# A two-block transformer step: the gated branch's score products in four parts, three of them inside the dense round that follows

## The chip, the cores and the metric

The kernel runs on one core of a Trainium2 chip. The metric is the device time of one execution, in microseconds. Full clock of TensorE is 2.4 GHz, and the profile gives the granted share of it.

## The reference

A first block (modulated norm, one input projection, a gated linear recurrence and a windowed attention side by side, output projection, 32-expert feed-forward with four experts a token) is followed by a second block of another kind. All in float32, 256 tokens, width 1024. The change touches only the gated recurrence of the first block, which works on chunks of 64 tokens and 4 heads of 128 keys:

```python
def step(state, inp):
    qc, kc, vc, lfc = inp
    b = jnp.cumsum(lfc, axis=-2)
    o_inter = jnp.einsum('bhck,bhkv->bhcv', qc * jnp.exp(b), state)
    rel = b[:, :, :, None, :] - b[:, :, None, :, :]
    decay = jnp.exp(jnp.where(causal, rel, -jnp.inf))
    scores = jnp.einsum('bhik,bhjk,bhijk->bhij', qc, kc, decay)
    o = o_inter + jnp.einsum('bhij,bhjv->bhiv', scores, vc)
    b_last = b[:, :, -1:, :]
    new_state = jnp.exp(b_last[:, :, 0, :])[..., None] * state + jnp.einsum(
        'bhjk,bhjv->bhkv', kc * jnp.exp(b_last - b), vc)
    return new_state, o
```

## The kernel before

Every engine has its own hand-written instruction stream, and semaphores join them. The dense projections of block 1 are *rounds* 0 to 15. A float32 weight is split into an upper part, made by ScalarE (`split_upper`, L356), and a lower part, made by VectorE (`split_lower`, L361); a matmul of the projection is then three products of rounded operands. Weights come in *pieces*. A round that is cut by columns has two pieces, j = 0 and j = 1, of 256 columns each; round 7 has pieces 13 and 14, round 8 has 15 and 16. Within a piece `split_cols` goes over two column groups c of 128, and for each over 8 contraction tiles and 3 products, so a round is 2 x 2 x 24 = 96 matmuls of 128x256. There are three places for upper parts, so ScalarE can make piece 16 only when TensorE has used piece 13.

Between rounds TensorE does the small work of the two branches, in the banks 4 to 6 of PSUM, taken in turn by `aux_bank()`. The consumer of each such bank waits on the count `aux_done`, and gives the bank back with `aux_free_V` or `aux_free_A`. Consumers take the banks in the order in which TensorE fills them.

The stretch of the change, on TensorE: the attention's value products; the gated branch's *score products* (64 products, for g in 8, i in 4, par in 2, each with 16 moving columns and 16 to 64 stationary columns, all into one bank, with one increment of `aux_done` behind the last); round 7; the transposes of the decayed keys (L1643, two banks); the products that make the chunk states (three banks, each waiting for `hg_kdT`); round 8; the products of scores and values.

The same stretch on VectorE, in order: the attention output (L2141, L2142), the gate (L2148, L2149), `split_lower(14)`, a memset of `st` (L2155), the masking of the scores from PSUM into `st` (L2161, 8 instructions, which waits for the scores' `aux_done`) with a memset that frees the bank (L2164), `split_lower(15)`, `split_lower(16)`, two copies of the transposed keys (L2170, `hg_kdT`) each with a memset (L2172), the states (L2178, L2181). `st` is first read by TensorE after round 8.

ScalarE makes the upper parts 15 and 16 in this stretch, then applies the sigmoid to the result of round 7 (L498) and makes the upper part 17. SyncE loads the weights; many of its loads wait for TensorE to be done with the slot (`big_done`, and in the expert stage `m1_up_done`, L989). Matmuls of float32 are recorded twice each in the profile; nearly all are recorded at the helper's line L563.

Of the kernel before, what the change touches and what calls it, by code (L numbers as in the profile page):

```python
# [31 lines left out]
CH, SUB = 64, 16  # L32
# [79 lines left out]
def program(nc, t, out):  # L112
    ctx = ExitStack()
    with ctx:
# [5 lines left out]
        def S(name):  # L120
            if name not in sems:
                sems[name] = ctx.enter_context(nc.semaphore(name))
            return sems[name]
# [31 lines left out]
        def at(m, name, lo=0, n=None, mem=arena):  # L155
            a, w = m[name]
            a = int(a * KB) + lo
            return mem[:, a:a + (n if n else int(w * KB) - lo)]
# [185 lines left out]
        hT_up = hT_r[:, :, :]  # L344
        hT_low = ring2_r[:, 1, 2048:4096].rearrange("p (k t) -> p k t", k=KD)
# [12 lines left out]
        def split_lower(v, n):  # L358
            v.wait_ge(S("w_upper"), n + 1)
            _, _, w, w_r = PIECES[n]  # L360
            nc.vector.tensor_tensor(w_r, w, upper(n), ALU.subtract).then_inc(S("w_lower"), 1)  # L361
# [75 lines left out]
        def banks(r):  # L437

            return slice(5, 7) if r == 0 else slice(2 * (r % 2), 2 * (r % 2) + 2)

        def kt_view(i):

            lo = 8 * SUB * i * (i + 1)
            return at(A1MAP, "kt", lo, 256 * (i + 1)).rearrange("p (g j) -> p g j", g=16)
# [117 lines left out]
        def mm(o, w, m, first, last):  # L562
            return nc.tensor.matmul(o, w, m, start=first, stop=last)  # L563
# [38 lines left out]
        def router_mm(w, ne, i, ks):  # L602
            for k in ks:
                last = mm(PS[:, 4 + i, 0:ne], hT[:, k, i * P:(i + 1) * P], w[:, k, :], k == 0, k == KD - 1)
            return last
# [836 lines left out]
        def _(pe):  # L1442
            aux = [0]

            def aux_bank():

                r = aux[0]
                aux[0] += 1
                if r >= 3:
                    wait(pe, aux_free(r - 3))  # L1450
                return PS[:, 4 + r % 3, :]

            def split_products(r, product, up, lo, ready, between=None):

                if r >= 2:
                    wait(pe, round_free(r - 2))
                ns = pieces_of(r)
                for j, n in enumerate(ns):
                    pe.wait_ge(S("w_lower"), n)
                    if ready:  # L1460
                        pe.wait_ge(S(ready), j + (1 if r < R2 else 3))
                    wu, wl = upper(n), PIECES[n][3]
                    last = product(j, ((up[j], wl), (lo[j], wu), (up[j], wu)), j == 0, j == len(ns) - 1)
                    last.then_inc(S("big_done") if j == len(ns) - 1 else S("half_done"), 1)
                    if between and j == 0:
                        between()
# [35 lines left out]
                                          n == 0 and m == 0 and k == 0, n == 1 and m == 2 and k == 3)  # L1502
                    last.then_inc(S("big_done") if n else S("half_done"), 1)

            def split_cols(r, up=hT_up, lo=hT_low, between=None):

                o = PS[:, banks(r), :].rearrange("p b (c t) -> p (b c) t", c=2)

                def product(j, parts, first, last):
                    nk, nc_ = parts[0][1].shape[1], parts[0][1].shape[2] // P  # L1510
                    for c in range(nc_):
                        for k in range(nk):
                            for m, (a, w) in enumerate(parts):
                                ins = mm(o[:, nc_ * j + c, :], w[:, k, c * P:(c + 1) * P], a[:, k, :],
                                         k == 0 and m == 0, k == nk - 1 and m == 2)
                    return ins
                split_products(r, product, (up, up), (lo, lo), None, between)

# [27 lines left out]
            for c in range(4):  # L1546
                last = nc.tensor.transpose(PS[:, 4, c * P:(c + 1) * P], modrow[:, 0, c * P:(c + 1) * P], ident)
# [5 lines left out]
            split_tokens(1)  # L1553
            keep_warm_short(6, 4)
            split_cols(2)
            ada(5)
            ada(6)
            split_cols(3)

            pe.wait_ge(S("consts"), 16)  # L1560
# [3 lines left out]
            for r in range(3):  # L1564
                o = aux_bank()
                for j in range(2):
                    for i in range(TT):
                        last = nc.tensor.transpose(o[:, (2 * j + i) * P:(2 * j + i + 1) * P], qk[:, i, 2 * r + j, :], ident)
# [5 lines left out]
            def att_score(o, hh, qtile, keys):  # L1574
                q = slice(64 * (hh % 2), 64 * (hh % 2) + 64)
                return mm(o, qkT[q, hh // 2, qtile * P:(qtile + 1) * P], qkT[q, 4 + hh // 4, 0:keys], True, True)


            o = [aux_bank() for _ in range(2)]
            for j in range(4):  # L1580
                for r in range(2):
                    last = att_score(o[r][:, j * P:(j + 1) * P], 2 * j + r, 0, P)
# [4 lines left out]
            for g in range(2):  # L1587
                o = [aux_bank() for _ in range(2)]
                for j in range(2):
                    for r in range(2):  # L1590
                        last = att_score(o[r][:, j * 256:(j + 1) * 256], 4 * g + r + 2 * j, 1, 256)
                        if j == 1:
                            last.then_inc(S("aux_done"), 1)
            split_tokens(5)
            ada(9)
            split_cols(6)
            ada(10)

            s = at(A1MAP, "s").rearrange("p (h n) -> p h n", h=AH)
            pe.wait_ge(S("att_p"), 1)  # L1600
            for b in range(3):
                for r in range(2):
                    o = aux_bank()
                    for j in range(4):
                        last = nc.tensor.transpose(o[:, j * P:(j + 1) * P], s[:, 4 * r + j, b * P:(b + 1) * P], ident)  # L1605
# [8 lines left out]
            for r in range(2):  # L1614
                o = aux_bank().rearrange("p (m t) -> p m t", m=2)
                for j in range(4):
# [3 lines left out]
                    last = mm(o[q, j // 2, P:256], vv[:, 1, kv], pT1[:, hh, :], False, True)  # L1620
# [2 lines left out]
            pe.wait_ge(S("hg_scores_in"), 1)  # L1623
            o = aux_bank().rearrange("p (g i) -> p g i", g=8)
            qt = at(A1MAP, "qt").rearrange("p (g i) -> p g i", g=16)
            for g in range(8):
                for i in range(4):
                    n = SUB * (i + 1)
                    for par in range(2):
                        hc, q0 = 2 * g + par, 64 * par  # L1630
                        last = mm(o[q0:q0 + n, g, SUB * i:SUB * i + SUB], kt_view(i)[:, hc, :],
                                  qt[:, hc, SUB * i:SUB * i + SUB], True, True)
            last.then_inc(S("aux_done"), 1)
            split_cols(7)

            pe.wait_ge(S("hg_kd"), 1)
            kd = at(A1MAP, "b").rearrange("p (h t) -> p h t", h=HH)
# [2 lines left out]
            for i in range(TT):  # L1640
                o = aux_bank()
                for hh in range(HH):
                    last = nc.tensor.transpose(o[:, hh * P:(hh + 1) * P], kd[:, hh, i * P:(i + 1) * P], ident)  # L1643
                last.then_inc(S("aux_done"), 1)

            for c in range(3):
                i, q = c // 2, slice(64 * (c % 2), 64 * (c % 2) + 64)
                o = aux_bank()
                pe.wait_ge(S("hg_kdT"), i + 1)
                for hh in range(HH):  # L1650
                    last = mm(o[:, hh * P:(hh + 1) * P], kdT[q, i, hh, :], vals[q, i, hh, :], True, True)
# [7 lines left out]
            for i in range(TT):  # L1659
                o = aux_bank()  # L1660
                pe.wait_ge(S("hg_state"), 2 * i + 1)
                halves = [(2 * i + par, slice(64 * par, 64 * par + 64)) for par in range(2)]
                for hh in range(HH):
                    for c, q in halves:
                        last = mm(o[q, hh * P:(hh + 1) * P], st[q, hh, i, :], vals[q, i, hh, :], True, c == 0)
                    for c, q in halves:
                        if c:
                            last = mm(o[q, hh * P:(hh + 1) * P], qb[:, hh, c * CH:(c + 1) * CH], states[:, c - 1, hh, :],
                                      False, True)
# [3 lines left out]
            o = aux_bank()  # L1673
            for c in range(4):
                last = nc.tensor.transpose(o[:, c * P:(c + 1) * P], modrow[:, 1, c * P:(c + 1) * P], ident)
# [4 lines left out]
            for r in range(2):  # L1680
                o = aux_bank()
                for j in range(2):
                    for i in range(TT):
                        last = nc.tensor.transpose(o[:, (2 * j + i) * P:(2 * j + i + 1) * P], ho[:, i, 2 * r + j, :], ident)
# [19 lines left out]
            for i in range(TT):  # L1704
                pe.wait_ge(S("hT_A"), 3 + i)
                last = router_mm(w_r1, NE, i, range(4, KD))
# [6 lines left out]
            for part in range(2):  # L1713
                for i in (part, part + 2):
                    for k in range(2):
                        c = P * k + CAP * (i // 2)
                        for tile in range(TT):
                            last = mm(PS[:, part, c:c + CAP], h[:, tile, 256 * i + k:256 * i + 256:2],
                                      selS[:, tile * CAP:(tile + 1) * CAP], tile == 0, tile == TT - 1)
# [66 lines left out]
            r = R2  # L1786
# [31 lines left out]
            for n in range(4):  # L1818
                o = aux_bank()
                for j in range(2):  # L1820
                    for i in range(TT):
                        last = nc.tensor.transpose(o[:, (2 * j + i) * P:(2 * j + i + 1) * P], qk2[:, i, 2 * n + j, :], ident)
# [20 lines left out]
            for hh in range(8):  # L1843
                if hh % 4 == 0:
                    pe.wait_ge(S("sb_sp"), hh // 4 + 1)
                o = aux_bank()
# [9 lines left out]
            for n in range(2):  # L1856
                pe.wait_ge(S("sb_w"), n + 1)
                o = aux_bank().rearrange("p (m t) -> p m t", m=2)
                for j in range(4):
# [3 lines left out]
                    last = mm(o[q, j // 2, P:256], v2[:, 1, hh * HD:(hh + 1) * HD], za[:, hh, 256:384], False, True)  # L1863
# [15 lines left out]
            for i in range(TT):  # L1879
                pe.wait_ge(S("hT_A"), 8 + i)  # L1880
                last = router_mm(w_r2, 36, i, range(4, KD))
# [731 lines left out]
```

## Time and profile before

| what | value |
|---|---|
| median of 3 runs (lowest, highest) | 1558.39 us (1557.97, 1558.5) |
| the profiled execution | 1558.42 us |
| its span, first to last instruction | 1556.6 us |
| TensorE matmul busy | 93% of the span |
| VectorE busy | 39% |
| ScalarE busy | 22% |
| mean granted clock of TensorE | 0.984 |

The page gives each engine's share of busy time and 40 slices of the span. The stretch of the change lies at 133 to 158 us, in the fourth slice and the start of the fifth; the first expert stage begins near 245 us.

### The profile page before, as it was taken

Reading aid. Unit: us, or ns where it says so; the run is one execution under the profiler, and the core shown is the slowest. Engines: PE = TensorE matmul, PEld = TensorE weight load, DVE = VectorE, ACT = ScalarE, POOL = GpSimd, SP = SyncE. Lnnn points to the kernel's source line nnn. Section 1 sums busy time; section 2 is a strip of 40 time slices with the busy share of each in tenths; the row PEclk is TensorE's granted clock in tenths of the full one; section 3 lists DMA queues with packets and bytes.
Section 4 is the critical chain, followed back from the end, with each engine's and each line's share of the span. In section 5 each row is a group of like instructions: output and inputs, shape, how many; then the busy total and the mean of one; then the engine's idle time right before and its main releaser. Section 6 shows DMA issues by size and latency. Waiting matters only on the chain.

```text
span 1556.6 us, 20902 instructions
## 1 busy us (share of the span) xinstructions
PE 1447.0 (93%) x8692; PEld 754.9 (48%) x8692; DVE 602.6 (39%) x920; ACT 342.8 (22%) x395; POOL 22.7 (1%) x36
## 2 busy tenths in 40 slices
PE   5999999999999999999998989999989999998677
PEld 2878985333333333333332333333338999854343
DVE  4686683232223232231321321323247687522111
ACT  4564332010101010110100100101033384321110
POOL 1100100000000000000000000000000000000000
PEclk9999999999999999999999999999999999999889
DMA  9986589999999999999999999999996446999998
GB/s 383 372 324 264 197 351 395 430 428 428 429 427 427 428 429 427 429 427 429 428 428 429 426 427 429 429 427 428 429 403 229 163 163 261 362 386 423 422 422 343
DMA packets 76385, 594.63 MB, mean 382 GB/s; under 512 B 5499, under 2 KB 6753, under 8 KB 36901
## 3 DMA queue, kind: packets, MB, share of 16 engines
q1 hardware_dynamic: 74000, 588.25, 91.5%
q0 software_dynamic: 1792, 4.86, 0.9%
q8 instruction: 48, 0.79, 0.2%
q10 hardware_dynamic: 532, 0.64, 0.1%
q14 instruction: 13, 0.10, 0.0%
HBM read 592.66 MB, written 1.06 MB: 381 GB/s over the span
## 4 chain that ended last, share of the span: by engine, by line
PE 60%; DMA 34%; DVE 3%; issue 1%; SPq 1%; ACT 1%; POOL 0%; DVEq 0%; ACTq 0%
PE PS L563 54%; DMA ring<-in_w_up 26%; DMA ring<-in_w_up_e 6%; PE PS L743 3%; DMA arena<-in_w_in 2%; DMA ring<-in_w_down_e 1%; PE PS L763 1%; PE PS L1528 1%; DVE ring_r L361 1%; DVE arena L853 1%; PE PS L679 1%; SPq L1093 1%; ACT ring_r L356 0%; POOL arena_r L1119 0%; PE PS L1605 0%
## 5 line engine op out<-in xcount | busy, mean ns | idle before, releaser
L563 PE MATMUL PS<-ring,arena 128*64 128x512 f32 x3020 | 671.2, 597 | 41.0 <-DMA ring<-in_w_up 28.7
L563 PEld LDWEIGHTS PS<-ring,arena 128*64 128x64 f32 x3020 | 212.3, 137 | 462.1 <-issue 400.1
L563 PE MATMUL PS<-arena 128*128 128x128 f32 (+12 forms) x1240 | 228.7, 441 | 2.9 <-DVE arena L2109 0.9
L841 DVE TENSOR_SCALAR arena<-PS 128x512 f32<-128x512 f32 x32 | 22.1, 692 | 482.6 <-PE PS L563 482.6
L542 ACT ACTIVATE arena<-arena 128x512 f32<-128x512 f32 x32 | 20.2, 630 | 698.5 <-DVE arena L841 698.5
L563 PE MATMUL PS<-ring_r 128*128 128x256 f32 (+1 forms) x576 | 171.6, 305 | 0.1
L563 PEld LDWEIGHTS PS<-arena 64*128 64x128 f32 (+6 forms) x1240 | 108.6, 164 | 120.4 <-issue 114.9
L563 PE MATMUL PS<-hT_r,ring_r 128*128 128x256 f32 x800 | 151.7, 286 | 0.3 <-DVE ring_r L361 0.3
L361 DVE TENSOR_TENSOR ring_r<-ring,ring_r 128x2048 fp32r<-128x2048 f32 x51 | 116.4, 2291 | 37.2 <-ACT ring_r L356 36.1
L563 PEld LDWEIGHTS PS<-hT_r,ring_r 128*128 128x128 f32 x800 | 127.8, 193 | 2.3 <-issue 1.4
L356 ACT ACTIVATE ring_r<-ring 128x2048 fp32r<-128x2048 f32 x51 | 97.2, 1912 | 104.6 <-PE PS L563 99.2
L563 PEld LDWEIGHTS PS<-ring_r 128*128 128x128 f32 x576 | 110.3, 192 | 5.2 <-DVE ring_r L2399 0.5
L563 PE MATMUL PS<-ring_r,hT_r 128*128 128x512 f32 (+1 forms) x336 | 99.3, 383 | 3.1 <-ACT hT_r L1212 1.7
L743 PE MATMUL PS<-ring,arena 128*32 128x256 f32 x896 | 61.6, 438 | 31.1 <-DMA ring<-in_w_up_e 24.4
L563 PEld LDWEIGHTS PS<-ring_r,hT_r 128*128 128x128 f32 x336 | 61.9, 188 | 18.4 <-issue 3.8
L835 DVE TENSOR_TENSOR x<-x,PS 128x2048 f32<-128x2048 f32 x31 | 70.6, 2278 | 0.0
L863 DVE TENSOR_TENSOR arena<-PS,arena 128x512 f32<-128x512 f32 x32 | 22.1, 691 | 118.3 <-PE PS L563 118.3
L743 PEld LDWEIGHTS PS<-ring,arena 128*32 128x32 f32 x896 | 32.1, 125 | 59.1 <-DMA ring<-in_w_up_e 23.6
L563 PE MATMUL PS<-arena_r,ring_r 128*128 128x256 f32 x352 | 45.2, 278 | 0.0
L853 DVE COPY arena<-PS 128x512 f32<-128x512 f32 x32 | 22.1, 691 | 55.7 <-PE PS L679 55.7
L563 PEld LDWEIGHTS PS<-arena_r,ring_r 128*128 128x128 f32 x352 | 43.2, 188 | 0.2 <-issue 0.2
L542 ACT ACT_TABLE_LOAD x31 | 39.8, 1283 | 1.1 <-issue 0.5
(382 smaller groups left out, 965.2 us busy)
## 6 DMA issues: line engine op xcount, KB each, us to landing
ring<-in_w_up SPq DMA_DIRECT2D x128, 2048.0 KB, 20.7
ring<-in_w_down SPq DMA_DIRECT2D x59, 2048.0 KB, 18.6
ring<-in_w_in SPq DMA_DIRECT2D x17, 2048.0 KB, 11.2
ring<-in_w_gate_e SPq DMA_DIRECT2D x14, 2048.0 KB, 19.3
ring<-in_w_down_e SPq DMA_DIRECT2D x13, 2048.0 KB, 20.1
ring<-in_w_up_e SPq DMA_DIRECT2D x13, 2048.0 KB, 19.0
ring<-in_w_ada SPq DMA_DIRECT2D x12, 2048.0 KB, 16.1
ring<-in_w_out SPq DMA_DIRECT2D x4, 2048.0 KB, 7.7
```

Of the source, the lines that this page charges most:

```text
L356: nc.scalar.activation(upper(n), PIECES[n][2], ACT.Copy).then_inc(S("w_upper"), 1)
L361: nc.vector.tensor_tensor(w_r, w, upper(n), ALU.subtract).then_inc(S("w_lower"), 1)
L542: nc.scalar.activation(sg, glu, ACT.Sigmoid, scale=1.702).then_inc(S(f"{X}_sg"), 1)
L563: return nc.tensor.matmul(o, w, m, start=first, stop=last)
L679: mm_ = nc.tensor.transpose(PS[:, 1, i * P:(i + 1) * P], actb[:, i * P:(i + 1) * P], ident)
L743: mm_ = nc.tensor.matmul(PS[q, 2 + i, 0:256], xg2[:, k * P + CAP2 * j:k * P + CAP2 * (j + 1)], moe2_weights(where, 2 * i + j // 2, j % 2, ...
L763: mm_ = nc.tensor.matmul(PS[q, b, :], aT2[:, kk * P + CAP2 * j:kk * P + CAP2 * (j + 1)], moe2_dst(where, 4 + j // 2)[:, 2 * (j % 2) + kk, ...
L835: V.tensor_tensor(xflat, xflat, PS[:, 4:8, :].rearrange("p b n -> p (b n)"), ALU.add).then_inc(S(f"{X}_added"), 1)
L841: V.tensor_scalar(glu.rearrange("p (kk b q) -> p kk b q", kk=4, b=2), hu[:, :, :, :, 0], 7.0, None, ALU.min)\
L853: V.tensor_copy(aT, PS[:, 1, :]).then_inc(S(f"{X}_aT"), 1)
L863: V.tensor_tensor(ye[:, 0:512], PS[:, 1, :], g2h, ALU.mult).then_inc(S(f"{X}_ye"), 1)
L1093: sp.dma_start(moe2_pair(2, i)[:, o, :].rearrange("p (k n) -> p k n", k=2)[:, kk, c], w[:, kk, :])\
```

## The change

The 64 score products stand in four parts of 16 (two values of g each). Part 0 stays ahead of round 7. Part 1 stands behind the first column group of round 7's piece 13, part 2 between the two pieces, part 3 behind the first column group of piece 14. The increment of `aux_done` is on the last product of part 3. The order of the instructions of all other engines is the same.

```diff
-            def split_cols(r, up=hT_up, lo=hT_low, between=None):
+            def split_cols(r, up=hT_up, lo=hT_low, between=None, after_column=None):
...
                             for m, (a, w) in enumerate(parts):
                                 ins = mm(o[:, nc_ * j + c, :], w[:, k, c * P:(c + 1) * P], a[:, k, :],
                                          k == 0 and m == 0, k == nk - 1 and m == 2)
+                        if after_column and c < nc_ - 1:
+                            after_column(j)
                     return ins
...
-            for g in range(8):
-                for i in range(4):
-                    n = SUB * (i + 1)
-                    for par in range(2):
-                        hc, q0 = 2 * g + par, 64 * par
-                        last = mm(o[q0:q0 + n, g, SUB * i:SUB * i + SUB], kt_view(i)[:, hc, :],
-                                  qt[:, hc, SUB * i:SUB * i + SUB], True, True)
-            last.then_inc(S("aux_done"), 1)
-            split_cols(7)
+            def hg_scores(part):
+
+                for g in range(2 * part, 2 * part + 2):
+                    for i in range(4):
+                        n = SUB * (i + 1)
+                        for par in range(2):
+                            hc, q0 = 2 * g + par, 64 * par
+                            last = mm(o[q0:q0 + n, g, SUB * i:SUB * i + SUB], kt_view(i)[:, hc, :],
+                                      qt[:, hc, SUB * i:SUB * i + SUB], True, True)
+                if part == 3:
+                    last.then_inc(S("aux_done"), 1)
+
+            hg_scores(0)
+            split_cols(7, between=lambda: hg_scores(2), after_column=lambda j: hg_scores(1 + 2 * j))
```

First place: TensorE before the change, where the score products end and round 7 begins. `arena` holds the scores' operands, `hT_r` and `ring_r` those of the dense round; 16x16 is stationary columns by moving columns.

```order
L563 MATMUL PS<-arena 64x128
L563 MATMUL PS<-arena 16x16 [waits aux_free_A,hg_scores_in]
L563 MATMUL PS<-arena 16x16
L563 MATMUL PS<-arena 32x16 x2
L563 MATMUL PS<-arena 48x16 x2
L563 MATMUL PS<-arena 64x16 x2
...
L563 MATMUL PS<-hT_r,ring_r 128x256 [waits w_lower,big_free_V]
L563 MATMUL PS<-ring_r 128x256
```

Second place: TensorE after the change, in the middle of round 7, from the last dense matmul of piece 13 over part 2 to the first of piece 14.

```order
L563 MATMUL PS<-hT_r,ring_r 128x256
L563 MATMUL PS<-arena 16x16 x2
L563 MATMUL PS<-arena 32x16 x2
L563 MATMUL PS<-arena 48x16 x2
L563 MATMUL PS<-arena 64x16 x2
...
L563 MATMUL PS<-hT_r,ring_r 128x256 [waits w_lower]
L563 MATMUL PS<-ring_r 128x256
```

Two groups g of scores stand between dense matmuls there, and likewise behind the first column group of either piece; before, all eight stood ahead of the round.

Third place: VectorE after the change, where it takes the scores and what is queued behind. L2168 is the mask (L2161 before), L361 the splits of pieces 15 and 16, L2177 the copy of the transposed keys (L2170 before).

```order
L2162 MEMSET arena 128x512
L2168 TENSOR_TENSOR arena<-PS,consts 16x8x16 [waits aux_done,v_step]
L2168 TENSOR_TENSOR arena<-PS,consts 32x8x16
...
L2171 MEMSET small 128x16 [waits hg_st]
L361 TENSOR_TENSOR ring_r<-ring,ring_r 128x8x256 [waits w_upper,aux_free_V]
L361 TENSOR_TENSOR ring_r<-ring,ring_r 128x8x256 [waits w_upper]
L2177 COPY arena<-PS 128x512 [waits aux_done]
```

Nothing moved here; what moved is the matmul that the first of these waits for, from ahead of round 7 to behind its third quarter.

## Rows read from the trace of the kernel before

**Rows 1.** The page: TensorE's share of the span, and its granted clock in 40 slices.

```profile
PE 1447.0 (93%) x8692; PEld 754.9 (48%) x8692; DVE 602.6 (39%) x920; ACT 342.8 (22%) x395; POOL 22.7 (1%) x36
...
PEclk9999999999999999999999999999999999999889
```

**Rows 2.** The chain of waits, 120 to 470 us: start, length, what.

```profile
133.57 20.23 PE PS L563 x256
...
155.12 31.48 PE PS L563 x272
...
367.82 25.10 DMA ring<-in_w_up
```

**Rows 3.** Timeline of TensorE, 131 to 158 us: start, length, operation, idle before.

```profile
136.30 4.30 PE L563 MATMUL PS<-arena 128*16 128x16 f32 x127
...
140.54 0.39 PE L563 MATMUL PS<-hT_r,ring_r 128*128 128x256 f32 x1
...
153.64 1.04 PE L1643 MATMUL PS<-consts,arena 128*128 128x128 f32 x8
155.11 2.23 PE L563 MATMUL PS<-arena 64*128 64x128 f32 x24 [0.44 <-DVE small L2172]
157.28 0.39 PE L563 MATMUL PS<-hT_r,ring_r 128*128 128x256 f32 x1
```

**Rows 4.** Windows inside round 7: length, busy PE, PEld, DVE, ACT, POOL, PEclk, DMA.

```profile
141.10:144.50 3.40, 3.40 (x18) 3.40 (x17) 3.31 (x6) 0.00 (x0) 0.00 (x0) 0.50 1.00 395
144.50:153.60 9.10, 9.10 (x78) 9.10 (x77) 5.68 (x8) 1.92 (x1) 0.00 (x0) 1.00 0.01 5
```

**Rows 5.** Timeline of TensorE around the small products after round 8.

```profile
168.65 0.28 PE L563 MATMUL PS<-ring_r 128*128 128x256 f32 x1
168.77 0.28 PE L563 MATMUL PS<-hT_r,ring_r 128*128 128x256 f32 x1
168.98 0.69 PE L563 MATMUL PS<-arena 64*64 64x128 f32 x5
...
174.83 0.39 PE L563 MATMUL PS<-hT_r,ring_r 128*128 128x256 f32 x1
175.05 0.28 PE L563 MATMUL PS<-ring_r 128*128 128x256 f32 x1
```

**Rows 6.** Timeline of VectorE, from the mask to the copy.

```profile
143.74 1.79 DVE L2161 TENSOR_TENSOR arena<-PS,consts 16x128 f32<-16x128 f32 x8
...
145.71 2.29 DVE L361 TENSOR_TENSOR ring_r<-ring,ring_r 128x2048 fp32r<-128x2048 f32 x1
150.09 2.29 DVE L361 TENSOR_TENSOR ring_r<-ring,ring_r 128x2048 fp32r<-128x2048 f32 x1 [2.09 <-ACT ring_r L356]
154.28 0.69 DVE L2170 COPY arena<-PS 128x512 f32<-128x512 f32 x1 [1.89 <-PE PS L1643]
```

**Rows 7.** Timeline of ScalarE in round 7.

```profile
148.14 1.92 ACT L356 ACTIVATE ring_r<-ring 128x2048 fp32r<-128x2048 f32 x1 [11.28 <-PE PS L563]
```

**Rows 8.** Idle times of TensorE elsewhere (timeline), and windows right behind each.

```profile
26.46 1.07 PE L1528 MATMUL PS<-ring,small 128*32 128x512 f32 x8 [3.05 <-DMA ring<-in_w_ada]
...
1499.01 1.42 PE L743 MATMUL PS<-ring,arena 128*32 128x256 f32 x16 [2.29 <-DMA ring<-in_w_gate_e]
...
1419.49 1.08 PE L743 MATMUL PS<-ring,arena 128*32 128x256 f32 x8 [4.53 <-DMA ring<-in_w_up_e]
...
26.50:30.00 3.50, 2.59 (x22) 1.08 (x23) 0.69 (x1) 0.84 (x1) 0.00 (x0) 1.00 1.06 389
...
1499.60:1503.00 3.40, 3.40 (x40) 1.74 (x32) 0.00 (x0) 0.00 (x0) 0.00 (x0) 0.50 1.02 424
...
1419.50:1424.50 5.00, 5.00 (x48) 2.35 (x52) 0.00 (x0) 0.00 (x0) 0.00 (x0) 0.50 1.01 423
```

**Rows 9.** A window at the first expert (last column GB/s), and SyncE's loads there.

```profile
250.00:255.00 5.00, 5.00 (x26) 1.61 (x24) 0.41 (x1) 0.00 (x0) 0.00 (x0) 1.00 0.79 265
...
250.86 11.09 SPq L989 DMA_DIRECT2D ring<-in_w_up  x4
```

## The prediction

> **What bounds the kernel now.** I read the page's slices first. TensorE is busy 93% of the span, and its clock row shows nines except near the end [rows 1]. Then the chain of waits over the first block: from 133.57 us it is TensorE's own matmuls for 20.23 us, then after two short links on VectorE again 31.48 us of matmuls, and only far inside the first expert stage does a DMA ring take over [rows 2]. So in the stretch of this change TensorE is the path, and VectorE stands in it at one point.
>
> Next, the timeline of TensorE. The score products run from 136.30 to 140.54 us, 4.24 us for eight groups of eight products (each recorded twice). Round 7 runs from 140.54 to 153.64, 13.10 us for 96 matmuls. Eight transposes follow, TensorE then stands idle 0.44 us for VectorE, the 24 records of the state products start at 155.11 and round 8 starts at 157.28 [rows 3]. The windows show why round 7 is slow: from 141.10 to 144.50 the granted clock was 0.50, i.e. 1.2 GHz, with TensorE busy all the time; after 144.50 it was 1.00, i.e. 2.4 GHz [rows 4]. What came before the fall were the small products, 16 columns each [rows 3].
>
> Does a microsecond saved or lost here reach the end? The queue of loads waits for TensorE: in 250 to 255 us the DMA engines were only 0.79 busy, and the loads of the second expert go out at 250.86, when the first expert's products free their slots [rows 9]. From there the weights run at full rate for most of the first expert stage. TensorE delayed by d before 250 us makes that gap d longer, so I pass d on one to one.
>
> **The change part by part.**
>
> *Clock (gain).* A round 7 matmul costs 0.12 us at full clock (168.65 to 168.77) [rows 5]. 96 of them are 11.52 us, and the first after small products costs 0.10 more (below): 11.62. Measured are 13.10 [rows 3], so 1.48 us went to the 3.4 us of half clock. After the change there are three stretches of about 3 us of dense matmuls between parts of 1.06 us (a quarter of 4.24), so no stretch is filled by small products alone. I take the fall as gone: -1.48. Bounds: -1.48 if it goes, 0 if it stays.
>
> *Switches (loss).* Dense to small costs 0.21 us instead of 0.12 (168.77 to 168.98), small to dense 0.22 instead of 0.12 (174.83 to 175.05) [rows 5]: +0.09 and +0.10. These are products of another tile size than the scores, the nearest rows there are. Three more pairs: +0.57. Bounds: 0 (weights loaded ahead hide it) and 6 x 0.28 = 1.7, if every switch costs a whole recorded matmul length (the x1 rows of [rows 5]). The Trainium skill, "TensorEngine Tiling (Array Packing)", Key Properties, says that a change of tiling mode drains TensorE; on that reading I would put the upper bound in the sum and the total would be 1.1 us longer. The rows show 0.09 and 0.10, so they decide.
>
> *TensorE up to the transposes.* Part 3 ends at 136.30 + 4.24 + 3 x (24 x 0.12 + 0.19) = 149.75. The last quarter takes 2.98, so the transposes start at 152.73 instead of 153.64 [rows 3]: 0.91 us early (1.48 - 0.57).
>
> *The signal of the scores (loss).* It comes with the last product of part 3, so at about 149.9 (the product's own 0.2 us behind its start), instead of ahead of round 7. Behind it on VectorE, in this order, stand the eight masking products (L2161, from 143.74), the weight split of piece 15 (ends 148.00), the split of piece 16 and the copy of the transposes (L2170) [rows 6]. Today VectorE masks at once, idles 2.09 us before piece 16, which needs ScalarE's part from 148.14 [rows 7], and 1.89 before the copy [rows 6]: 3.98 us of slack. The mask starts 149.9 - 143.74 = 6.16 us late, and more than the slack is used up. In full: 149.9 + (148.00 - 143.74 = 4.26) = 154.16; split 16 with 0.04 for the step, 156.49; the copy at 156.53 instead of 154.28. ScalarE's part of piece 16 waits for the first half of round 7, which now ends near 144.5 instead of near 148, so it isn't what is waited for. Piece 14, needed by the second half of round 7 at 145.6, is split ahead of the mask, so before 143.74, and is in time.
>
> *The new wait.* The state products started 0.83 us after the copy (155.11 - 154.28), so now at 157.36: **2.25 us later**. TensorE finishes its transposes at 153.77 and idles 3.6 us where it idled 0.44 [rows 3]. The gain of 0.91 falls into this idle time and is lost; the early end of round 7 is worth nothing. State products and round 8 follow as before, 2.25 us late; ScalarE's gate (after round 7) and SyncE's load into the freed slot come 0.9 us earlier and wait for nobody. VectorE's later splits (17, 18) are wanted a whole round later and are hidden by it.
>
> *A new fall of the clock (loss).* The rows with idle time: after 3.05 us idle the clock stayed at 1.00, after 2.29 it was 0.50, after 4.53 it was 0.50 [rows 8]. 3.6 us lies between the 3.05 that held and the 4.53 that fell, and the state products behind it are small too, the very sort of work before today's fall. I take it that it falls. Its price by today's: 1.48 in 3.4 us, 0.44 per us. If 1.3 us of it lie on state products (0.09 us each, 24 of them, which lose perhaps 0.2) and 2.1 on dense matmuls (0.9), it is +1.1. Bounds 0 (no fall) and 1.5 (all of it dense).
>
> **Sum.** +2.25 + 1.1 = +3.3 us. The profiled execution took 1558.42 us, its span 1556.6, and the median is 1558.39, so nothing needs converting: 1558.4 + 3.3 = 1561.7 us, 0.21% slower. What a measurement of this kernel can tell is about 0.2%, 3.1 us, or 1561.5. So the forecast stands just on the edge.
>
> **The rivals.**
>
> *B, the wait without the fall.* TensorE idles, but the clock holds as it did after 3.05 us [rows 8]: +2.25, 1560.6 us. For it: the idle time is nearer to 3.05 than to 4.53. Against: it held there before full-size matmuls, and 2.29 us was enough elsewhere.
>
> *C, not slower: the lateness is absorbed.* It needs the mask to finish early enough. If the scores' signal came by 149.9 - (156.53 - 153.37) = 146.7 us, the copy would follow the transposes at once (154.28 - 0.91 = 153.37) and the kernel would be 0.9 us faster, 1557.5 us. That is the point from which it decides; three quarters of round 7 would have to fit into 6 us, against 9 by the rows. Or the wait happens, but the waits of TensorE for weights in the expert stage take it up (the chain's 25.10 us on a DMA ring [rows 2]): 1558.4. Against that speaks the gap in the DMA at 250 us [rows 9].
>
> *D, the change doesn't do what it says.* Its purpose on the clock fails, the half clock stays inside round 7. Then scores come 1.5 us later, so does the copy: +3.7, 1562.1 us, and with a second fall after the idle time 1563.2.
>
> *E, the switches empty the array.* Then each costs a whole recorded matmul. Five of the six switches lie before the signal at 0.28 instead of about 0.095, +0.9 on the signal: 1561.5 without a fall, 1562.6 with it. The 0.21 and 0.22 us of [rows 5] speak against it. The page named above is the one that states such a rule.
>
> **How the numbers follow.** Forecast A (wait and fall) 0.43, B 0.27, C 0.12, D 0.08, E 0.05, something else 0.05. The predicted time is A's, 1561.7. The range takes in all of A to E but D's second fall: 1557.4 to 1563.0. Slower by over 0.2%: a little over half of A (it sits on the edge), D, most of E, some of the rest: 0.42. Faster by over 0.2% needs more than 3.1 us, which no case gives: 0.03. Within 0.2%: 0.55.
>
> **What would show it.** Right: the clock is 1.00 through round 7; four groups of score products of 1.06 us; VectorE's mask starts at 149.9 after an idle time of 6 us put down to TensorE; TensorE idles 3 to 4 us for VectorE before the state products; after it a stretch at 0.50. Wrong: an idle time under 1 us there (C), clock 1.00 after it (B), a stretch at 0.50 inside round 7 (D), quarters of round 7 over 3.3 us apart (E). If round 8 starts near 159.5 and the end is still at 1558.4, passing the delay on was the error.

## The result and the profile after

The change is slower: 1566.85 us median of 5 runs (1564.56 to 1568.27) against 1558.39 (1557.55 to 1560.83) of the kernel before in the same comparison, ratio 1.0053 with a 95% interval of 1.0042 to 1.0064. The forecast was 1561.7 in a range of 1557.4 to 1563.0. The direction was right, the size was not: +8.5 us instead of +3.3. The profiled execution of the changed kernel took 1566.85 us, its span 1565.1.

Lines of this profile are those of the changed file: L2155 is VectorE's gate product (L2148 before), L2168 the mask (L2161), L2177 the copy of the transposed keys (L2170), L2179 its memset (L2172), L1650 the transposes (L1643).

The timeline of TensorE, from two windows, which answers to [rows 3]; rows of single dense matmuls are left out.

```profile
139.81 0.58 PE L563 MATMUL PS<-hT_r,ring_r 128*128 128x256 f32 x1 [2.21 <-DVE arena L2155]
...
144.27 1.13 PE L563 MATMUL PS<-arena 128*16 128x16 f32 x32
...
148.39 1.13 PE L563 MATMUL PS<-arena 128*16 128x16 f32 x32
...
152.51 1.13 PE L563 MATMUL PS<-arena 128*16 128x16 f32 x32
...
156.54 1.04 PE L1650 MATMUL PS<-consts,arena 128*128 128x128 f32 x8
161.08 4.08 PE L563 MATMUL PS<-arena 64*128 64x128 f32 x24 [3.51 <-DVE small L2179]
...
165.09 0.58 PE L563 MATMUL PS<-hT_r,ring_r 128*128 128x256 f32 x1
```

Four things are to be seen. Ahead of round 7 TensorE now idles 2.21 us for VectorE's gate product; before, there was no such row. The parts stand 4.12 us apart, as forecast (1.06 + 3.07). Ahead of the state products TensorE idles 3.51 us (before 0.44). And the 24 records of the state products take 4.08 us instead of 2.23. Round 8 starts at 165.09 instead of 157.28, and the small products behind it at 177.57 instead of 168.98 [rows 5].

The timeline of VectorE, which answers to [rows 6].

```profile
138.53 1.22 DVE L2155 TENSOR_TENSOR arena<-PS,arena 128x1024 f32<-128x1024 f32 x1
139.79 1.23 DVE L2156 TENSOR_TENSOR arena<-arena,small 128x1024 f32<-128x1024 f32 x1
141.05 2.29 DVE L361 TENSOR_TENSOR ring_r<-ring,ring_r 128x2048 fp32r<-128x2048 f32 x1
143.40 0.48 DVE L2162 MEMSET arena<- 128x512 f32 x1
153.75 1.79 DVE L2168 TENSOR_TENSOR arena<-PS,consts 16x128 f32<-16x128 f32 x8 [9.88 <-PE PS L563]
155.61 0.07 DVE L2171 MEMSET small<- 128x16 f32 x1
155.72 4.49 DVE L361 TENSOR_TENSOR ring_r<-ring,ring_r 128x2048 fp32r<-128x2048 f32 x2
160.24 0.69 DVE L2177 COPY arena<-PS 128x512 f32<-128x512 f32 x1
```

VectorE's gate product ends at 139.75, and the first dense matmul starts right behind it, at 139.81. Before, it ended at 139.58, while TensorE was still at the score products (until 140.54 [rows 3]):

```profile
138.36 1.22 DVE L2148 TENSOR_TENSOR arena<-PS,arena 128x1024 f32<-128x1024 f32 x1
```

After the change VectorE waits 9.88 us for the scores; the two splits run back to back behind the mask, and the copy comes at 160.24 instead of 154.28.

The windows (columns as in [rows 4]) show where the clock was down.

```profile
140.00:145.00 5.00, 5.00 (x48) 4.79 (x48) 3.79 (x3) 0.00 (x0) 0.00 (x0) 0.70 0.93 371
145.00:150.00 5.00, 5.00 (x74) 4.72 (x69) 0.00 (x0) 1.45 (x1) 0.00 (x0) 1.00 0.02 7
...
160.00:165.00 5.00, 3.92 (x24) 3.82 (x24) 3.24 (x10) 0.00 (x0) 0.00 (x0) 0.51 0.74 299
165.00:170.00 5.00, 5.00 (x35) 4.91 (x35) 4.54 (x10) 0.00 (x0) 0.00 (x0) 0.81 0.01 3
```

The half clock in round 7 is still there, and a second one covers the state products and the start of round 8.

The path of the 8.5 us, from these rows: the stretch starts 0.17 late; +2.2 for the gate product; +0.6 for three pairs of switches, with the half clock in round 7 costing what it cost before, so the transposes are 2.90 late (156.54 against 153.64). Then +3.07 more idle time (3.51 - 0.44), so the state products are 5.97 late (161.08 - 155.11); +1.84 because they run at half clock, so round 8 starts 7.81 late (165.09 - 157.28); and the rest of the half clock on dense matmuls, about 0.8, makes 8.6, as the 177.57 against 168.98 behind round 8 shows (8.59). SyncE's first load for the second expert goes out at 259.46 us, against 250.86 [rows 9], which is 8.6 again.

```profile
259.46 0.36 SPq L989 DMA_DIRECT2D ring<-in_w_up  x1
```

So passing a delay on one to one up to here was right, and 8.46 of it are in the measured medians. It is right behind here too, within 2.5 us: from that load to the end the profiled executions of this study take 1306.3 to 1308.8 us, but for the second profile of before with 1310.5.

### The profile page after: what moved, and what is told of

It is laid out like the page before. It is cut to its first block, busy times and chain, and to the rows that moved or that the text cites. A ratio compares the mean times of both kernels' runs of the same rounds, so it can differ in the third digit from the quotient of the medians.

```text
span 1565.1 us, 20902 instructions
## 1 busy us (share of the span) xinstructions
PE 1454.6 (93%) x8692; PEld 760.5 (49%) x8692; DVE 601.9 (38%) x920; ACT 342.8 (22%) x395; POOL 22.7 (1%) x36
## 3 DMA queue, kind: packets, MB, share of 16 engines
HBM read 592.66 MB, written 1.06 MB: 379 GB/s over the span
## 4 chain that ended last, share of the span: by engine, by line
PE 59%; DMA 34%; DVE 4%; issue 1%; ACT 1%; SPq 0%; DVEq 0%; ACTq 0%
PE PS L563 53%; DMA ring<-in_w_up 25%; DMA ring<-in_w_up_e 7%; PE PS L743 3%; DMA ring<-in_w_ada 1%; DVE ring_r L361 1%; PE PS L1530 1%; PE PS L763 1%; DVE arena L853 1%; PE PS L679 1%; ACT ring_r L356 0%; PE PS L1607 0%; DVE arena L2131 0%; DVE ring_r L2017 0%; DVE small L2122 0%
## 5 line engine op out<-in xcount | busy, mean ns | idle before, releaser
L361 DVE TENSOR_TENSOR ring_r<-ring,ring_r 128x2048 fp32r<-128x2048 f32 x51 | 116.3, 2291 | 36.6 <-ACT ring_r L356 35.5
```

## The experiments

Ratios are to the kernel before, run in between on the same chip. Single runs of one kernel lie up to 8.5 us apart (1555.16 to 1563.69), so the intervals reach 1.3 to 3.0 us to either side, and the mechanism is read from the profiles. The runs were made in three comparisons, with medians of before of 1558.07 (gate first, splits first, both, one late), 1558.9 (two then six, halves, halves with the gate) and 1558.96 us (filled, gate only, halves with the gate again). A kernel's loss is counted against the median of its own comparison; the change's loss is the 8.46 us above.

### The gate product first

```diff
+            v.wait_ge(S("sig_g"), 1)
+            gs = at(A1MAP, "gs")
+            o = begin(5)
+            sig(TV(gs, o.rearrange(flat), gs, ALU.mult), "big_free_V")
             for r in range(2):
                 o = aux_bank().rearrange("p (m t) -> p m t", m=2)
                 L(CP(att_up[:, 2 * r:2 * r + 2, :], o))
...
-            v.wait_ge(S("sig_g"), 1)
-            gs = at(A1MAP, "gs")
-            o = begin(5)
-            sig(TV(gs, o.rearrange(flat), gs, ALU.mult), "big_free_V")
```

> The changed kernel with VectorE's gate product (L2155 of it), which frees the banks that round 7 writes, ahead of the two attention output copies instead of behind them. Theory: part 0 alone doesn't cover the wait for these banks, and that idle time made the clock fall inside round 7. Then the wait of 2.2 us and the half clock of 1.4 us go, the transposes start near 152.8, VectorE's mask near 150.0, and TensorE still idles 3 to 4 us before the state products: 1561.8 to 1563.3 us, 3.5 to 5 us better than the change and that much worse than before. Rival (small products make the clock fall whether or not TensorE idles): half clock stays in round 7 and it is 1.4 us longer, 1563.2 to 1564.7.

Measured: 1566.93 us median (1562.55 to 1567.44), ratio 1.0042 (1.0023 to 1.0061). Its timelines of TensorE and of VectorE:

```profile
140.70 1.13 PE L563 MATMUL PS<-arena 128*16 128x16 f32 x32
...
152.97 1.04 PE L1650 MATMUL PS<-consts,arena 128*128 128x128 f32 x8
157.51 4.08 PE L563 MATMUL PS<-arena 64*128 64x128 f32 x24 [3.51 <-DVE small L2179]
```

```profile
150.19 1.79 DVE L2168 TENSOR_TENSOR arena<-PS,consts 16x128 f32<-16x128 f32 x8 [6.24 <-PE PS L563]
...
156.68 0.69 DVE L2177 COPY arena<-PS 128x512 f32<-128x512 f32 x1
```

The bank wait is gone and the clock is up in round 7: the transposes start at 152.97, the mask at 150.19. These are within 0.3 us the times of the prediction (152.73, 149.9, 156.53 for the copy, 157.36 for the state products), so its working was that of a kernel without the bank wait. But the median is 8.9 us above before and above what either theory expected, and so the time alone shows no gain. The five runs lie at 1562.55 and 1563.49 and at 1566.93 to 1567.44, and the profiled one (1567.3) is of the second sort. In it the second half clock lasts until 166.4, 4.9 us into round 8 (in the change 1.8 us):

```profile
157.00:161.00 4.00, 3.49 (x23) 3.52 (x24) 2.27 (x8) 0.00 (x0) 0.00 (x0) 0.50 0.73 300
161.00:164.00 3.00, 3.00 (x14) 2.77 (x14) 2.79 (x11) 0.00 (x0) 0.00 (x0) 0.50 0.00 0
164.00:168.00 4.00, 4.00 (x27) 4.00 (x26) 2.18 (x2) 0.00 (x0) 0.58 (x1) 0.70 0.03 6
```

At the eight transposes ahead of the router, which start at 236.23 us here, at 238.45 in the change and at 229.86 before, this execution is still 2.2 us better than the change. A fall of the clock in the router's small products behind them takes 1.3 of that.

### The splits of pieces 15 and 16 ahead of the mask

```diff
+            split_lower(v, 15)
+            split_lower(v, 16)
             st = at(A1MAP, "st")
...
-            split_lower(v, 15)
-            split_lower(v, 16)
```

> The changed kernel with VectorE's splits of pieces 15 and 16 ahead of the mask, so that only the mask stands between the scores and the copy of the transposed keys. Theory: the wait of TensorE before the state products (3.5 us) comes from these two splits queued behind the late scores, and the second half clock (6.8 us long) comes from that wait. Then the copy follows the transposes at once, the clock stays up, and what is left is the lateness of 2.9 us at the transposes: 1561.3 us. Rival (the second fall comes from the small state products or from work before): the clock still falls near 160 and it ends near 1564.

Measured: 1561.14 us (1559.48 to 1565.64), ratio 1.0019 (1.0008 to 1.0030), as the theory had it. TensorE:

```profile
140.16 0.39 PE L563 MATMUL PS<-hT_r,ring_r 128*128 128x256 f32 x1 [2.21 <-DVE arena L2155]
...
155.49 1.03 PE L1650 MATMUL PS<-consts,arena 128*128 128x128 f32 x8
157.40 2.23 PE L563 MATMUL PS<-arena 64*128 64x128 f32 x24 [0.87 <-DVE small L2179]
```

The bank wait is unchanged, the idle time before the state products falls from 3.51 to 0.87 us and these take 2.23 us again. This one reorder takes back 5.4 of 8.5 us (the loss is 3.07 us, 1561.14 against 1558.07, instead of 8.46). With the same 2.21 us of idle time, round 7 kept its clock here.

### Both

The two edits above together.

> The gate first and the splits first together. Theory: both waits and both falls of the clock are gone and the switches are paid: transposes at 152.8 instead of 153.6, 1557.5 us, 0.9 us better than before. Rival (the parts cost more than the switches seen, or another wait comes): 1559 us or more.

Measured: 1559.51 us (1557.28 to 1563.69), ratio 1.0012 (1.0001 to 1.0024): all but 1.4 us of the loss is gone, but the 0.9 us gain isn't there, and the time is on the rival's side (1559 or more). The transposes start at 153.27, and the idle time is 0.86. The gain was counted against a profile of before whose clock had fallen in round 7; the second profile of before, below, shows that it doesn't always. Against one where it holds, three pairs of switches (0.6) and 0.4 us more idle time make about +1, and the first load for the second expert goes out at 250.92, 1.05 behind that second profile's 249.87.

### One group late

The edit is shown against the changed kernel. From here on `hg_scores` takes the groups g, and a second argument that puts the signal on the last product.

```diff
-            hg_scores(0)
-            split_cols(7, between=lambda: hg_scores(2), after_column=lambda j: hg_scores(1 + 2 * j))
+            hg_scores(range(7))
+            split_cols(7, after_column=lambda j: hg_scores(range(7, 8), True) if j else None)
```

> The kernel before with one change: of the eight groups of scores seven stand ahead of round 7 and the eighth behind the first column group of piece 14, with the signal on it. No bank wait (seven groups end at 140.0, the banks are free at 139.6), the clock falls inside round 7 as before. It isolates the late signal. Theory: the signal comes near 151.3, VectorE's copy of the keys near 157.9, TensorE idles about 3 us before the state products and the clock falls there: 1562.5 to 1565 us. Rival (the late signal is harmless, the uncovered bank wait does all): 1558.7 us.

Measured: 1563.65 us (1561.34 to 1565.65), ratio 1.0035 (1.0025 to 1.0045), inside the theory's range.

```profile
149.14 0.60 PE L563 MATMUL PS<-arena 128*16 128x16 f32 x16
...
152.63 1.04 PE L1650 MATMUL PS<-consts,arena 128*128 128x128 f32 x8
157.18 4.09 PE L563 MATMUL PS<-arena 64*128 64x128 f32 x24 [3.51 <-DVE small L2179]
```

With no bank wait and a single pair of switches more, one late group of eight is enough for the idle time of 3.51 us, the half clock on the state products and 5.6 us. The clock stayed up in round 7, with seven groups of small products in a row ahead of it.

### The kernel before, profiled again

> The kernel before, unchanged, for a second profile. Theory: the half clock inside round 7 (141.1 to 144.5 in its first profile) depends on when the chip looks, since one_late has 3.7 us of the same small products ahead of round 7 and its clock stayed up. Then a second profile may show round 7 at full clock, 11.6 us instead of 13.1, with the transposes 1.5 us earlier against the start of the scores, and the end near 1556.5. Rival: it falls every time, 13.1 us again, and the 0.5 us of small products less in one_late are what counted.

Measured: one run of 1560.38 us. The start of its attention products (133.50 in the first profile), its transposes, and the windows over round 7:

```profile
133.98 7.11 PE L563 MATMUL PS<-arena 128*64 128x256 f32 x160
...
152.63 1.04 PE L1643 MATMUL PS<-consts,arena 128*128 128x128 f32 x8
```

```profile
141.00:145.00 4.00, 4.00 (x37) 3.98 (x34) 3.88 (x7) 0.00 (x0) 0.00 (x0) 1.00 1.00 397
145.00:152.00 7.00, 7.00 (x60) 7.00 (x60) 5.65 (x8) 1.92 (x1) 0.00 (x0) 1.00 0.02 6
```

The clock held, and the transposes start at 152.63 although the stretch began 0.48 later. So the half clock in round 7 of [rows 4], on which the -1.48 of the prediction rests, is not a fixed part of the kernel before. The end wasn't near 1556.5, as expected, but 2.0 us behind the first profile's. This execution is 1.0 us ahead of the first one until 1343 us. Then a fall of the clock that the first one doesn't have costs it 1.4 us (granted clock 0.66 over 1343 to 1348, against 1.00), and behind it a wait for a load of 6.1 us instead of 4.5 costs the rest. In all thirteen profiles of this study the clock is down in round 7 in three: the first of before, the change's, and that of the kernel with the idle time filled.

### Two groups ahead, six behind the first column group

```diff
+            hg_scores(range(2))
+            split_cols(7, after_column=lambda j: None if j else hg_scores(range(2, 8), True))
```

> Two groups of scores ahead of round 7, the other six behind the first column group of piece 13, with the signal on them. The bank wait is uncovered as in the change, but the signal comes near 146 and VectorE's slack of 4 us should take it. It isolates the bank wait. Theory: TensorE idles 2.2 us for the gate product, and nothing before the state products but the old 0.4: 2.2 + 0.2 for one more pair of switches, less up to 1.5 if the clock stays up: 1559.0 to 1560.5 us. Rival (the bank wait does more than its own length, through the clock): 1562 or more.

Measured: 1561.92 us (1558.41 to 1565.02), ratio 1.0018 (1.0008 to 1.0028), 3.0 us above the baseline of that comparison, 1558.9. That misses the theory's range by 1.4 us and ends just under the rival's 1562.

```profile
139.93 0.39 PE L563 MATMUL PS<-hT_r,ring_r 128*128 128x256 f32 x1 [2.21 <-DVE arena L2155]
...
156.37 2.23 PE L563 MATMUL PS<-arena 64*128 64x128 f32 x24 [0.44 <-DVE small L2179]
```

The mask comes 2.36 us after VectorE is ready for it, and its slack takes that. The profile speaks for the theory: the clock holds through round 7, the transposes start at 154.90, and from the start of the attention products to them it takes 2.46 us longer than in the second profile of before, which is 2.21 for the wait and 0.2 for the switches. So the bank wait alone costs its own length and the switches in this profile; the 0.6 us more of the medians is within what they carry. Its 3.0 us and the 5.6 of one_late add up to 8.6, the change's loss.

### Halves, and halves with the gate first

```diff
+            hg_scores(range(4))
+            split_cols(7, after_column=lambda j: None if j else hg_scores(range(4, 8), True))
```

> Four groups ahead of round 7, four behind its first column group. The bank wait is then half covered (part ahead ends 138.4, banks free at 139.6: 1.2 us idle), the signal comes near 145. Theory: 1.2 + 0.2 less up to 1.5 for the clock: 1557 to 1559.5 us, no wait before the state products. Rival: 2 us slower than before, if the clock falls in round 7 in spite of it.

Measured: 1559.96 us (1557.18 to 1563.75), ratio 1.0009 (0.9998 to 1.0020). The time is half a microsecond over the theory's range. The idle time ahead of round 7 is 1.15 us: what part of the score products stands ahead sets how much of the wait is covered (2.21 with two groups, 1.15 with four, none with eight).

> The same halves with VectorE's gate product first, so the bank wait is gone. Theory: only one more pair of switches (0.2 us) against the kernel before, and the clock up in round 7: 1.3 us better than a run of before whose clock falls there, 0.2 worse than one whose clock holds: 1556.8 to 1558.5 us, no difference that can be measured. Rival: parts lose time in a way not seen yet, 1560 or more.

Measured: 1557.67 us (1556.14 to 1561.37, 12 runs), ratio 0.9991 (0.9982 to 0.9999), inside the theory's range of times. To see whether the gain is real:

> The kernel with halves and the gate first a second time, since its 0.9991 (0.9982 to 0.9999) is near one. Theory: a pair of switches (+0.2 us) against a fall of the clock in round 7 that before shows in one of its two profiles (half of 1.5): ratio 0.9990 to 1.0000. Rival: the first result was chance, 1.0000 to 1.0010.

Measured: 1557.66 us (1555.16 to 1563.69), ratio 0.9996 (0.9985 to 1.0006). And with the gate product first in the kernel before and nothing else:

> The kernel before with VectorE's gate product moved ahead of the attention output copies, and nothing else. Theory: it moves no wait that TensorE feels before the change (round 7's banks are free at 139.6, wanted at 140.5): no difference, ratio within 0.9990 to 1.0010. Rival: it is this and not the halves that gives the 0.09% of halves_gate: ratio 0.999 or less.

Measured: 1558.95 us against 1558.96, ratio 1.0000 (0.9991 to 1.0010). The moved gate does nothing by itself. Halves with the gate first is as fast as the kernel before; a gain under 0.1% may be there and isn't shown.

### The idle time filled

```diff
                 last.then_inc(S("aux_done"), 1)
+            keep_warm(4, 0)

             for c in range(3):
                 i, q = c // 2, slice(64 * (c % 2), 64 * (c % 2) + 64)
```

> The changed kernel with four throw-away products of 128x512 (identity times constants, into a bank that round 8 overwrites) between the transposes and the state products, where TensorE idles 3.5 us. They are extra work that the output doesn't need. Both waits stay; only the idle time is filled. Theory: the idle time is what makes the clock fall near 160. Then it stays up, the 24 state products take 2.2 us instead of 4.1 and round 8 starts at full clock: about 2.6 us better than the change, 1564 us. Rival (small state products or the late start bring the fall): no better than the change, 1567 us.

Measured: 1565.95 us (1565.11 to 1567.52), ratio 1.0042 (1.0029 to 1.0056). That lies between the theory's 1564 and the rival's 1567 and decides nothing. The profile does:

```profile
156.25 1.04 PE L1650 MATMUL PS<-consts,arena 128*128 128x128 f32 x8
157.12 3.60 PE L563 MATMUL PS<-consts 128*128 128x512 f32 x8
160.79 2.23 PE L563 MATMUL PS<-arena 64*128 64x128 f32 x24
```

```profile
157.00:161.00 4.00, 3.93 (x13) 1.69 (x12) 3.87 (x5) 2.28 (x2) 0.00 (x0) 1.00 0.83 289
...
163.00:168.00 5.00, 5.00 (x43) 5.00 (x43) 4.79 (x12) 0.00 (x0) 0.00 (x0) 1.00 0.06 23
```

The state products start as late as in the change (160.79 against 161.08) and take 2.23 us: with the idle time filled the clock stays up, so it is the idle time that brings it down there, not the small products behind it. At the transposes ahead of the router (235.53 us, 238.45 in the change) this execution is 2.9 us ahead of the change's; 0.3 of that it had at its start, so the expected 2.6 us are there. They don't reach the end: the loss in the medians is 7.0 us instead of 8.5, and the two intervals overlap. In this profile the clock fell at 243 us, in the router's small products, for 10.2 us, and by SyncE's first load for the second expert (261.06 against 259.46) the execution has lost 4.5 us against the change. The filler alone isn't behind that fall: halves_gate, its second run, gate_only and gate_first had one at 236 to 245 us too. These four have the gate product first, as does `both`, which had none; of the eight other profiles only this one had it. Whether the moved gate product has a part in it is open (gate_only's median is that of before), and so is whether the fall hides the gain in the other runs of this kernel.

## Why the prediction was wrong

- **Passing on a delay to the end**: right. 8.6 us behind round 8, 8.6 at SyncE's first load of the second expert, 8.46 in the medians.
- **Switches**, +0.57 for three pairs: right; parts are 4.12 us apart against 4.13. The Trainium skill, "TensorEngine Tiling (Array Packing)", Key Properties, says that a change of tiling mode drains TensorE. Read as a whole recorded matmul for each switch, that would have made the parts 4.5 us apart (an estimate from the 0.28 us of [rows 5]), and the rows disagree with that reading.
- **TensorE up to the transposes**: here is the step that failed, by leaving a term out. "So no stretch is filled by small products alone" looked at the clock only. The prediction never asked what the score products ahead of round 7 were covering. The row of the order in front of it says so: round 7's first matmul waits for `big_free_V`, which VectorE's gate product gives at 139.6 to 139.8 us. Before, the score products ran until 140.54 and hid it; a quarter of them ends at 137.6. This cost 2.2 us. The profile of gate_first shows it, which has no such wait and all the predicted times up to the state products to within 0.3 us, and so do the times of two_then_six, which has the wait and not the late signal, and is 3.0 us slower than before. The median of gate_first (8.9 us above before) doesn't show it.
- **Clock, -1.48**: a gain that wasn't there. It was down in round 7 of the changed kernel's profile too, which made the signal and all behind it about 1.5 us later than forecast, and it was up in a second profile of the kernel before. One profile can't tell a fall that belongs to the kernel from one that comes in some executions.
- **The signal of the scores and the new wait**: right in its mechanism, VectorE's queue behind the late mask. Idle time 3.51 us in three kernels, 3.6 forecast. In the change all of it stands 3.7 us later (copy at 160.24 instead of 156.53), by the bank wait and the half clock in round 7.
- **The new fall of the clock**: right that it falls, mis-sized at +1.1; it cost 2.6. The prediction gave it 3.4 us, 1.3 of them on state products that "lose perhaps 0.2". In the change it covers all 4 us of the state products, which lose 1.84, and 1.8 us of dense matmuls, 0.8 more. The price of 0.44 us per us was right for both (1.84 in 4.01 us is 0.46, with 0.17 us a product instead of 0.093); the 0.2 was too low by that very price, and the length was too short. In gate_first it lasted longer still, 4.9 us into the dense matmuls.
- **The row that spoke for a held clock**: [rows 8] has 3.05 us of idle time at 26 us after which the clock stayed up, and B leans on it. All thirteen profiles have that idle time (3.05 to 3.07 us), and in eight of them the clock is at 0.50 for 3.4 us or more right behind it, the second profile of before among them. One profile showed the rarer case.
- **Rivals**: B (no fall), C (absorbed) and E (4.12 us apart, not 4.5) are out. D came true in part, the half clock stayed in round 7, but it was not the main loss.

In one sum: 3.3 us forecast, 2.2 for the bank wait that was put at nothing, 1.5 for the half clock in round 7 that was taken as gone, and 1.5 for the second fall are 8.5. That the direction came out right is owed to the late signal, which the prediction had; the bank wait, the half clock that stayed and the longer fall made it a clear loss instead of one on the edge of what can be told.

## To carry to other kernels

Before work is moved out of a place, list the semaphores that the instruction behind it waits for and when each is given: the work may be the cover of a wait that shows nowhere in the profile. Where part of a small job is made late, ask what is queued on the consumer's engine behind its last piece; moving two independent splits ahead of the mask won back 5.4 us here. A stretch at half clock in one profile is a reason to take a second profile, before a change is built on it.

## What was not expected of the hardware

In all three profiles with 3.51 us of idle time the clock was down before the idle time was over. With 3.05 us, at 26 us, it fell in eight of thirteen, and with 2.21 us ahead of round 7 in two of four; but ahead of round 7 it also fell once in three profiles without any idle time, behind all eight groups of score products, so what part the 2.21 us have in it is open. At half clock, products of 128 columns on half the rows slowed from 0.093 to 0.17 us, close to a factor of two, while dense ones went from 0.12 to 0.21. And the same kernel's clock may fall in one execution and hold in the next: in round 7, or in the router's small products at 236 to 245 us, where it cost 4.5 us in the profile of halves_gate (its matmuls stand 1.4 us ahead of those of before until then, and 3.1 behind after it) and 1.3 in those of gate_only and gate_first.
